# Output groups begun inside the gates' stage, and the next part's first two products begun inside each part of a feed-forward

## The chip, the cores and the metric

One core of a Trainium2 chip runs the whole program. The metric is device microseconds (us) of one execution, the median over several; the profile is of one execution more. TensorE is PE in the rows, VectorE DVE, ScalarE ACT, GpSimd POOL, SyncE SP.

## What is computed

Two transformer blocks follow each other on 1,024 tokens of width 1,024. The first has two layers. Each layer projects its input, runs four kinds of attention side by side, multiplies their joined output by a gate, projects it and normalises:

```python
for l in range(DEPTH):                      # DEPTH = 2
    proj = jnp.einsum('bsd,dc->bsc', h_res, w_in[l])
    ...
    mixed = jnp.concatenate([_merge(out_fox), _merge(out_sb), _merge(out_mla), _merge(out_mem)], axis=-1)
    y = jnp.einsum('bsc,cd->bsd', mixed * jax.nn.silu(gate), w_out[l])
    h_res = _layer_norm(DEEPNORM_ALPHA * h_res + y, ln_g[l], ln_b[l])
```

The second block has one layer, with window attention, a recurrent mixer and at the end a feed-forward of inner width 4,096:

```python
h = rms_norm(x, norm_ffn_pre[l]) * (1.0 + sc2) + sh2
f = jnp.square(jax.nn.relu(h @ w_ff1[l])) @ w_ff2[l]
x = (x + gt2 * rms_norm(f, norm_ffn_post[l])).astype(x.dtype)
```

## The kernel before

Every large product is made of three: both factors are split into a rounded high part and a low part (value minus high), and `split_gemm` (L202 to L210) adds high by high, high by low and low by high into one PSUM bank. A sum over the eight channel tiles of 128 is thus 24 matmuls. Weights come from HBM in chunks of 1 MB, by SP's queue; POOL splits each (a CAST at L193 and a TENSOR_TENSOR at L195 for the first block, L3959 and L3961 for the feed-forward).

The program is a row of stages, each an `nc.Block()`: every engine has its own instruction list for the stage, and the stage ends with a barrier at which all five engines meet. No engine starts on the next stage's list before all have come to the end of this one. SP's list opens with the clearing of the previous stage's semaphores, then issues the stage's first loads. Inside a stage the order is written out by hand, and semaphores that count finished groups tie the engines together.

**The gates' stage** (`gate_stage`, L2031, once per layer). TensorE makes 16 groups g of 24 matmuls with 512 columns: chunk c = g // 4 has four groups, tile g // 2 % 2 by half g % 2 (a half is 512 tokens), into bank g % 4. ACT takes the sigmoid of the bank (L2079), DVE multiplies it by the bank (L2094, `gated`), then into `mixed` (L2096), ACT rounds the product to `mixed_high` (L2075), and DVE makes `mixed_low` (L2088), two groups behind. SP loads the chunks C_GATE + 2, C_GATE + 3, C_OUT and C_OUT + 1 after 4, 8, 12 and 16 groups; POOL splits all but the last, which is left to the next stage.

**The edge** (`boundary`, L1178, after each layer). Out groups g = 0 to 31 (`do_out`, L1351) are 24 matmuls of 256 columns each: column chunk c = g // 4 % 4, token tile t = 4 * (g // 16) + g % 4, into bank g % 4. DVE adds each to the residual x (`add`, L1457). Here x was put away in HBM during the layer, since its place in SBUF was used for other things, and its two halves of 2 MB are the first loads of the stage (L1284). What gates group 4 is this:

```python
def room(g):
    if g >= 4:
        pe.wait_ge(*evacuated(g - 4))      # DVE's add(g - 4), which waits for x
...
if g < 16 and g % 4 == 0 and c == 1:
    pe.wait_ge(w_split, 1)                 # POOL's split of C_OUT + 1, in this stage
```

Later in the stage come statistics, normalisation (L1481, L1482) and the turn to channel-major, paced by those adds.

**The feed-forward** (`feed_forward`, L4121) runs in four parts of 1,024 inner channels, a stage each (`ffn_part`). Upward: 16 groups of 24 matmuls with 512 columns into banks g % 4, four groups to a weight chunk; groups 4 and on wait for `moved`, ACT's relu of the group four before (L4279), and each fourth for `wsplit`, POOL's split of its chunk. DVE squares (L4223) and splits. Downward: 32 groups of 12 matmuls in banks 0 to 7; DVE adds them into x_residual_two (L4235 in the first part, L4237 later; `added`). At the end of a part SP loads chunks 0 and 1 of the next (chunk 1 only when all downward groups are done), and POOL splits chunk 0, but not chunk 1. The stage before the feed-forward, `mix_out`, ends with `ffn.begin_up(0)` and `ffn.begin_up(1)`: seven of the eight channel tiles of upward groups 0 and 1, 21 matmuls each. Only the first part uses that (`begun = KT - 1 if first and g < 2`); its groups 0 and 1 are the last 3 matmuls each.

Of the kernel before, what the change touches and what calls it, by code (L numbers as in the profile page):

```python
# [31 lines left out]
P = 128  # L32
# [1145 lines left out]
def boundary(k, a, last, b):  # L1178
# [99 lines left out]
    with nc.Block() as block:  # L1278
# [63 lines left out]
        @block.tensor  # L1342
        def _(pe):
            if mem:
                pe.wait_ge(const_here, 16)

            def room(g):
                if g >= 4:
                    pe.wait_ge(*evacuated(g - 4))

            def do_out(g):  # L1351
                c, t = out_group(g)
                if g < 16 and g % 4 == 0 and c == 1:
                    pe.wait_ge(w_split, 1)
                room(g)
                gemm(nc, bank(g, 256), over_columns(last, C_OUT + c, t, 0, 256, last.mixed_high, last.mixed_low)).then_inc(products, 1)

            def do_turn(half, c):
                n = 8 * half + c
                pe.wait_ge(normed, 4 * half + 4)  # L1360
                if n >= 4:
                    pe.wait_ge(split, n - 3)
                for i in range(4):
                    mm = nc.tensor.transpose(k.psum[:, 4 + n % 4, i * P:(i + 1) * P], x[:, 4 * half + i, c * P:(c + 1) * P], k.ident)
                mm.then_inc(turned, 1)

            def do_fox(n):
                kind = fox[n][0]
                room(n_out + n)
                if kind == "logit":  # L1370
                    c, to, pairs = C_FL, bank(n_out + n)[0:FORGET_COLS, :], over_tokens(b, C_FL, 0, FORGET_COLS, fox[n][1])
                elif kind == "value":
                    c, to, pairs = C_FV, bank(n_out + n, 256), over_columns(b, C_FV, fox[n][1], 0, 256)
                else:
                    c, to = C_FQ if kind == "query" else C_FK, bank(n_out + n)
                    pairs = over_tokens(b, c, fox[n][1] * P, P, fox[n][2])
                if n < 9:
                    pe.wait_ge(w_split, (1 if last else 0) + (C_FL, C_FQ, C_FK, C_FV).index(c) + 1)
                pe.wait_ge(split, 8 if n < 9 else 16)
                gemm(nc, to, pairs).then_inc(products, 1)  # L1380

            def do_mem():
                for c in range(KT):
                    pe.wait_ge(mem_ready, 2)
                    if c >= 4:
                        pe.wait_ge(mem_moved, c - 3)
                    for t in range(2):
                        mm = nc.tensor.transpose(k.psum[:, 4 + c % 4, t * P:(t + 1) * P], mem_x[:, t, c * P:(c + 1) * P], k.ident)
                    mm.then_inc(mem_turned, 1)

            def turn_vectors():
                pe.wait_ge(rows_here, 16 * (len(vector_rows(a, vec_rows)) + 1))
                nc.tensor.transpose(k.psum[:, 4, 0:98], vec_rows, k.ident[0:98, 0:98]).then_inc(vec_turned, 1)
                nc.tensor.transpose(k.psum[:, 5, 0:32], mod_rows, k.ident[0:32, 0:32]).then_inc(vec_turned, 1)

            def turn_mix(n):
                (t0, t1), c = mix_units[n]
                pe.wait_ge(diagonal_ready, t1)
                if n >= 2:
                    pe.wait_ge(*mix_moved(n - 2))  # L1400
                for i, t in enumerate(range(t0, t1)):
                    mm = nc.tensor.matmul(k.psum[:, 6 + n % 2, i * P:(i + 1) * P], x[:, t, c * P:(c + 1) * P], diagonals[:, t, :],
                                          start=True, stop=True)
                mm.then_inc(mix_turned, 1)

            for g in range(n_out):
                if b and 22 <= g < 30:
                    do_turn(0, g - 22)
                if not b and g == 8:
                    turn_vectors()  # L1410
                if not b and 23 <= g < 31:
                    turn_mix(g - 23)
                do_out(g)
            if not b:
                for n in range(8, len(mix_units)):
                    turn_mix(n)
            if b:
                if not last:
                    for c in range(KT):
                        do_turn(0, c)  # L1420
                for n in range(9):
                    if n >= 4:
                        do_turn(1, n - 4)
                    do_fox(n)
                for c in range(5, KT):
                    do_turn(1, c)
                for n in range(9, len(fox)):
                    if mem and n == 12:
                        do_mem()
                    do_fox(n)  # L1430
# [600 lines left out]
def gate_stage(k, b, tag):  # L2031
    nc, W = k.nc, b.W
    mixed = b.mixed
    st = Stage(k, "gate" + tag)
    names = ("products_done", "sigmoid_ready", "gated", "dve_step", "weights_rounded", "weights_split", "mixed_rounded")
    products, sigmoid, gated, step, rounded, split, mixed_rounded = (st.sem(n) for n in names)
    n_groups = 2 * NT
    with nc.Block() as block:  # L2038
        @block.sync
        def _(sp):  # L2040
            st.clear_previous(sp)
            W.load(sp, C_OUT + 2)
            W.load(sp, C_OUT + 3)
            for n in range(4):

                sp.wait_ge(products, 4 * (n + 1))
                W.load(sp, C_GATE + 2 + n)

        @block.tensor
        def _(pe):  # L2050
            for g in range(n_groups):
                c = g // 4
                if g % 4 == 0 and c >= 2:

                    pe.wait_ge(split, c + 1)
                if g >= 4:

                    pe.wait_ge(gated, g - 3)
                gemm(nc, k.bank(g % 4), over_tokens(b, C_GATE + c, g // 2 % 2 * P, P, g % 2)).then_inc(products, 1)

        @block.gpsimd
        def _(pool):
            def used(c):
                if c < C_OUT + 2:
                    pool.wait_ge(products, 4 * (c - 2 - C_GATE + 1))
            W.split(pool, (C_OUT + 2, C_OUT + 3, C_GATE + 2, C_GATE + 3, C_OUT), rounded, split, used)

        def part_of(x, g):
            return x[:, g // 2, g % 2 * HALF:(g % 2 + 1) * HALF]

        @block.scalar
        def _(act):
            def round_high(g):
                act.wait_ge(step, g + 1)
                nc.scalar.copy(part_of(b.mixed_high, g), part_of(mixed, g)).then_inc(mixed_rounded, 1)  # L2075

            for g in range(n_groups):
                act.wait_ge(products, g + 1)
                nc.scalar.activation(part_of(b.gate_sigmoids, g), k.bank(g % 4), ACT.Sigmoid).then_inc(sigmoid, 1)  # L2079
                if g:  # L2080
                    round_high(g - 1)
            round_high(n_groups - 1)

        @block.vector
        def _(dve):
            def subtract(g):
                dve.wait_ge(mixed_rounded, g + 1)
                nc.vector.tensor_tensor(part_of(b.mixed_low, g), part_of(mixed, g), part_of(b.mixed_high, g), ALU.subtract)  # L2088

            for g in range(n_groups):  # L2090
                s = part_of(b.gate_sigmoids, g)
                part = part_of(mixed, g)
                dve.wait_ge(sigmoid, g + 1)
                nc.vector.tensor_tensor(s, s, k.bank(g % 4), ALU.mult).then_inc(gated, 1)  # L2094
                dve.wait_ge(gated, g + 1)
                nc.vector.tensor_tensor(part, part, s, ALU.mult).then_inc(step, 1)  # L2096
                if g >= 2:
                    subtract(g - 2)
            subtract(n_groups - 2)
            subtract(n_groups - 1)  # L2100
# [2020 lines left out]
def feed_forward(k, ffn, post, out):  # L4121
# [8 lines left out]
    def ffn_part(part, which):  # L4130
# [22 lines left out]
        with nc.Block() as block:  # L4153
# [33 lines left out]
            def _(pe):  # L4187

                for g in range(2 * KT):
                    if g % 4 == 0 and g:  # L4190
                        pe.wait_ge(wsplit, g // 4)
                    if g >= 4:

                        pe.wait_ge(moved, g - 3)
                    begun = KT - 1 if first and g < 2 else 0
                    split_gemm(nc, k.bank(g % 4), [ffn.up_product(g, i) for i in range(begun, KT)], first=not begun).then_inc(up_done, 1)

                for n in range(2):
                    for r in range(2):
# [4 lines left out]
                        for t in (4, 5, 6, 7, 0, 1, 2, 3) if not n and not r else range(NT):  # L4204
                            if not n and not r and t == 0:
                                pe.wait_ge(moved, 16)
                            if n and not r:
# [2 lines left out]
                            split_gemm(nc, k.bank(t), [((hid_high[:, 4 * r + i, tok], hid_low[:, 4 * r + i, tok]),  # L4210
                                                        weights(c, i, 0, HALF)) for i in range(4)],
                                       first=(r == 0), last=(r == 1)).then_inc(down_done, 1)

            @block.vector
            def _(dve):
# [119 lines left out]
```

## Time and profile before

| what | value |
|---|---|
| median of 3 runs | 3958.15 us (3957.75 to 3960.38) |
| the profiled execution's own time | 3959.55 us |
| its span, first to last instruction | 3957.7 us |
| granted TensorE clock, mean | 0.971 of full |
| TensorE busy | 93 % |
| VectorE busy | 44 % |
| ScalarE busy | 29 % |
| GpSimd busy | 18 % |
| data moved | 225.78 MB, 57 GB/s mean |

Shares are of the span. The 1.85 us between span and time lie around the recorded instructions. A matmul's busy time is longer than the distance to the next one's start, since matmuls are pipelined; what a group takes is its count by the distance of starts. A wait "<-PEq L2038" is idle time of TensorE that ended with its own sequencer's instruction on that line, here the barrier at a stage's end.

### The profile page before, as it was taken

What the parts mean: (1) busy time and instruction counts of PE and PEld (TensorE: products, weight loads), DVE (VectorE), ACT (ScalarE), POOL (GpSimd) and SP (SyncE); (2) the same over time, 40 slices, a digit from 0 to 9 for tenths busy, and PEclk for the clock granted to TensorE, in tenths of its full rate; (3) what the DMA queues carried; (4) which work ended last, traced back from release to release, by engine and by line L of the source; (5) the groups of instructions that cost most, each with busy time, mean ns of one, the idle gap of its engine ahead of it and who ended that gap; (6) DMA issues with size and microseconds to landing.
All of it is one profiled execution on the core that took longest, in us unless ns stands there. A gap on an engine that the chain in (4) does not pass through costs nothing. (4 is left out here: it accounts for less than half of the span.)

```text
span 3957.7 us, 67331 instructions
## 1 busy us (share of the span) xinstructions
PE 3693.3 (93%) x29462; PEld 2793.7 (71%) x29462; DVE 1733.6 (44%) x3002; ACT 1154.9 (29%) x2208; POOL 710.9 (18%) x248
## 2 busy tenths in 40 slices
PE   6899998998999989899889999998999999999998
PEld 5664667886646678778667777776687568887876
DVE  6645546456445364531774555454003253223143
ACT  2436333114363331201644444443110121001011
POOL 2110003121100041122011111110221012322321
PEclk9999899999998999999999999999899999999999
DMA  4131201221212012312110010000213211111112
GB/s 154 46 94 40 64 14 62 76 75 51 89 40 65 16 60 76 129 43 73 51 37 19 25 30 25 25 30 18 80 56 93 86 43 43 54 43 54 43 59 101
DMA packets 190189, 225.78 MB, mean 57 GB/s; under 512 B 20990, under 2 KB 168000, under 8 KB 187080
## 3 DMA queue, kind: packets, MB, share of 16 engines
q1 hardware_dynamic: 189896, 221.47, 16.9%
q8 instruction: 233, 3.82, 0.4%
q14 instruction: 60, 0.49, 0.0%
HBM read 188.89 MB, written 32.56 MB: 56 GB/s over the span
## 5 line engine op out<-in xcount | busy, mean ns | idle before, releaser
L193 POOL CAST weights_high<-weights_value 128x2048 fp32r<-128x2048 f32 x34 | 66.3, 1949 | 1260.9 <-DMA weights_value<-in_w_in_dram 1017.3
L208 PE MATMUL banks<-h_high,weights_high 128*128 128x512 f32 x608 | 242.5, 399 | 8.1 <-PEq L830 5.1
L208 PE MATMUL banks<-h_high,weights_low 128*128 128x512 f32 x608 | 239.3, 394 | 0.0
L208 PE MATMUL banks<-ffn_in_high,ffn_weights_high 128*128 128x512 f32 x512 | 202.7, 396 | 3.4 <-PEq L4153 3.1
L208 PE MATMUL banks<-ffn_in_low,ffn_weights_high 128*128 128x512 f32 x512 | 202.3, 395 | 0.0
L208 PE MATMUL banks<-ffn_in_high,ffn_weights_low 128*128 128x512 f32 x512 | 202.2, 395 | 0.0
L208 PE MATMUL banks<-ffn_weights_high,hidden_high 128*128 128x512 f32 x512 | 199.2, 389 | 0.0
L208 PE MATMUL banks<-ffn_weights_low,hidden_high 128*128 128x512 f32 x512 | 199.2, 389 | 0.0
L208 PE MATMUL banks<-ffn_weights_high,hidden_low 128*128 128x512 f32 x512 | 199.2, 389 | 0.0
L4279 ACT ACTIVATE hidden_value<-banks 128x512 f32<-128x512 f32 x64 | 38.3, 599 | 547.7 <-PE banks L208 547.6
L208 PE MATMUL banks<-h_high_again,pair_weights_high 128*128 128x512 f32 x384 | 179.5, 467 | 7.1 <-PEq L2318 7.1
L3959 POOL CAST ffn_weights_high<-ffn_weights_value 128x2048 fp32r<-128x2048 f32 x32 | 60.7, 1897 | 622.9 <-DMA ffn_weights_value<-in_w_ff_dram 445.0
L195 POOL TENSOR_TENSOR weights_low<-weights_value,weights_high 128x2048 fp32r<-128x2048 f32 x34 | 161.6, 4752 | 2.7
L4223 DVE TENSOR_TENSOR hidden_value<-hidden_value 128x512 f32<-128x512 f32 x64 | 71.2, 1114 | 200.1 <-ACT hidden_value L4279 200.1
L208 PE MATMUL banks<-weights_high,mixed_high 128*128 128x256 f32 x512 | 148.3, 290 | 8.4 <-PEq L2038 8.4
L850 PE MATMUL banks<-keys,queries 64*128 64x512 f32 (+3 forms) x512 | 110.8, 550 | 47.2 <-ACT attention_scratch L968 41.8
L208 PE MATMUL banks<-h_split_low,pair_weights_high 128*128 128x512 f32 x384 | 152.6, 397 | 0.0
L3961 POOL TENSOR_TENSOR ffn_weights_low<-ffn_weights_value,ffn_weights_high 128x2048 fp32r<-128x2048 f32 x32 | 151.7, 4739 | 2.6
L208 PE MATMUL banks<-h_high_again,pair_weights_low 128*128 128x512 f32 x384 | 150.4, 392 | 0.0
L208 PE MATMUL banks<-weights_high,h_high 128*128 128x256 f32 (+1 forms) x512 | 145.3, 284 | 1.9 <-PEq L625 1.9
L208 PE MATMUL banks<-weights_low,mixed_high 128*128 128x256 f32 x512 | 146.6, 286 | 0.0
L208 PE MATMUL banks<-weights_high,second_low 128*128 128x256 f32 (+1 forms) x512 | 145.0, 283 | 0.0
(481 smaller groups left out, 9148.1 us busy)
## 6 DMA issues: line engine op xcount, KB each, us to landing
ffn_weights_value<-in_w_ff_dram SPq DMA_DIRECT2D x32, 1024.0 KB, 5.2
weights_value<-in_w_in_dram SPq DMA_DIRECT2D x24, 1024.0 KB, 5.2
attention_scratch<-in_ada_w_dram SPq DMA_DIRECT2D x12, 1024.0 KB, 5.2
pair_weights_value<-in_w_in_dram SPq DMA_DIRECT2D x24, 512.0 KB, 4.0
ndow_weights_value<-in_w_in_dram SPq DMA_DIRECT2D x10, 1024.0 KB, 5.2
weights_value<-in_w_out_dram SPq DMA_DIRECT2D x8, 1024.0 KB, 5.0
gates_value<-in_w_in_dram SPq DMA_DIRECT2D x16, 512.0 KB, 4.6
first_mixed<-in_ada_w_dram SPq DMA_DIRECT2D x6, 1024.0 KB, 5.3
```

Of the source, the lines that this page charges most:

```text
L193: nc.gpsimd.tensor_copy(high, value).then_inc(rounded, 1)
L195: nc.gpsimd.tensor_tensor(low, value, high, ALU.subtract).then_inc(done, 1)
L208: mm = nc.tensor.matmul(out, x, y, start=(first and i == 0 and j == 0), stop=(last and i == n - 1 and j == 2))
L850: mm = nc.tensor.matmul(slot(e, at + done, size), q(p, e, t), key(p, e, done * P, (done + size) * P), start=True, stop=turned_part is None)
L3959: nc.gpsimd.tensor_copy(high[:], value[:]).then_inc(rounded, 1)
L3961: nc.gpsimd.tensor_tensor(low[:], value[:], high[:], ALU.subtract).then_inc(split, 1)
L4223: nc.vector.tensor_tensor(place(hid_value, g), place(hid_value, g), place(hid_value, g), ALU.mult).then_inc(squared, 1)
L4279: nc.scalar.activation(place(hid_value, g), k.bank(g % 4), ACT.Relu).then_inc(moved, 1)
```

## The change

In the gates' stage the groups of a chunk change places: both tiles of half 0 come first, then both of half 1, and `part_of` follows. After group 15 TensorE goes on, in the same stage, with 21 of the 24 matmuls (channel tiles 0 to 6) of out groups 0 to 3, into banks 0 to 3 with 256 columns. It waits for the split of C_OUT (`split`, 5), for `mixed_low` of group 12 (a new semaphore `mixed_split`, 13) and for each bank's gating. In the edge's stage groups 0 to 3 keep their last 3 matmuls each. In the feed-forward each part but the last ends with `begin_up` of the next part's groups 0 and 1, after waits for the split of the next chunk 0 (`wsplit`, 8) and for DVE's adds of banks 0 and 1, and all four parts start groups 0 and 1 with the last 3 matmuls. No load, no split and no other engine's work changes, except that SP clears one semaphore more per layer. The number of matmuls is the same.

```diff
--- before.py
+++ after.py
@@ -1353,7 +1353,9 @@
                 if g < 16 and g % 4 == 0 and c == 1:
                     pe.wait_ge(w_split, 1)
                 room(g)
-                gemm(nc, bank(g, 256), over_columns(last, C_OUT + c, t, 0, 256, last.mixed_high, last.mixed_low)).then_inc(products, 1)
+                begun = KT - 1 if g < 4 else 0
+                split_gemm(nc, bank(g, 256), over_columns(last, C_OUT + c, t, 0, 256, last.mixed_high, last.mixed_low)[begun:],
+                           first=not begun).then_inc(products, 1)
 
             def do_turn(half, c):
                 n = 8 * half + c
@@ -2032,8 +2034,8 @@
     nc, W = k.nc, b.W
     mixed = b.mixed
     st = Stage(k, "gate" + tag)
-    names = ("products_done", "sigmoid_ready", "gated", "dve_step", "weights_rounded", "weights_split", "mixed_rounded")
-    products, sigmoid, gated, step, rounded, split, mixed_rounded = (st.sem(n) for n in names)
+    names = ("products_done", "sigmoid_ready", "gated", "dve_step", "weights_rounded", "weights_split", "mixed_rounded", "mixed_split")
+    products, sigmoid, gated, step, rounded, split, mixed_rounded, mixed_split = (st.sem(n) for n in names)
     n_groups = 2 * NT
     with nc.Block() as block:
         @block.sync
@@ -2056,7 +2058,12 @@
                 if g >= 4:
 
                     pe.wait_ge(gated, g - 3)
-                gemm(nc, k.bank(g % 4), over_tokens(b, C_GATE + c, g // 2 % 2 * P, P, g % 2)).then_inc(products, 1)
+                gemm(nc, k.bank(g % 4), over_tokens(b, C_GATE + c, g % 2 * P, P, g // 2 % 2)).then_inc(products, 1)
+            pe.wait_ge(split, 5)
+            pe.wait_ge(mixed_split, n_groups - 3)
+            for t in range(4):
+                pe.wait_ge(gated, n_groups - 3 + t)
+                split_gemm(nc, k.bank(t, 256), over_columns(b, C_OUT, t, 0, 256, b.mixed_high, b.mixed_low)[:KT - 1], last=False)
 
         @block.gpsimd
         def _(pool):
@@ -2066,7 +2073,8 @@
             W.split(pool, (C_OUT + 2, C_OUT + 3, C_GATE + 2, C_GATE + 3, C_OUT), rounded, split, used)
 
         def part_of(x, g):
-            return x[:, g // 2, g % 2 * HALF:(g % 2 + 1) * HALF]
+            tile, half = g // 4 * 2 + g % 2, g // 2 % 2
+            return x[:, tile, half * HALF:(half + 1) * HALF]
 
         @block.scalar
         def _(act):
@@ -2085,7 +2093,8 @@
         def _(dve):
             def subtract(g):
                 dve.wait_ge(mixed_rounded, g + 1)
-                nc.vector.tensor_tensor(part_of(b.mixed_low, g), part_of(mixed, g), part_of(b.mixed_high, g), ALU.subtract)
+                nc.vector.tensor_tensor(part_of(b.mixed_low, g), part_of(mixed, g), part_of(b.mixed_high, g),
+                                        ALU.subtract).then_inc(mixed_split, 1)
 
             for g in range(n_groups):
                 s = part_of(b.gate_sigmoids, g)
@@ -4192,7 +4201,7 @@
                     if g >= 4:
 
                         pe.wait_ge(moved, g - 3)
-                    begun = KT - 1 if first and g < 2 else 0
+                    begun = KT - 1 if g < 2 else 0
                     split_gemm(nc, k.bank(g % 4), [ffn.up_product(g, i) for i in range(begun, KT)], first=not begun).then_inc(up_done, 1)
 
                 for n in range(2):
@@ -4210,6 +4219,11 @@
                             split_gemm(nc, k.bank(t), [((hid_high[:, 4 * r + i, tok], hid_low[:, 4 * r + i, tok]),
                                                         weights(c, i, 0, HALF)) for i in range(4)],
                                        first=(r == 0), last=(r == 1)).then_inc(down_done, 1)
+                if not last:
+                    pe.wait_ge(wsplit, 8)
+                    for g in range(2):
+                        pe.wait_ge(added, NT + g + 1)
+                        ffn.begin_up(g)
 
             @block.vector
             def _(dve):
```

TensorE's list at the end of the first gates' stage, before; the branch is the end of the stage's list, and the next one waits for the barrier:

```order
L208 MATMUL banks<-second_low,weights_high 128x512
L208 MATMUL banks<-h_high,weights_low 128x512
L2038 UNCONDITIONAL_BRANCH
L1342 UNCONDITIONAL_BRANCH [waits barrier_Pool_Activation_PE_DVE_SP_release]
L208 MATMUL banks<-weights_high,mixed_high 128x256
```

and with the change. The names of semaphores that the listing prints are those of the first stage that had the same numbers; the waits here are for `split`, `mixed_split` and `gated`:

```order
L208 MATMUL banks<-second_low,weights_high 128x512
L208 MATMUL banks<-h_high,weights_low 128x512
L208 MATMUL banks<-weights_high,mixed_high 128x256 [waits fox_0_late_values_done,fox_0_scaled,fox_0_act_moved]
L208 MATMUL banks<-weights_low,mixed_high 128x256
L208 MATMUL banks<-weights_high,first_low 128x256
```

Out group 0 has moved ahead of the barrier. Its and its three followers' 84 matmuls end here, at what is left of group 0 behind the barrier:

```order
L208 MATMUL banks<-weights_low,mixed_high 128x256
L208 MATMUL banks<-weights_high,first_low 128x256
L2040 UNCONDITIONAL_BRANCH
L1342 UNCONDITIONAL_BRANCH [waits barrier_Pool_Activation_PE_DVE_SP_release]
L208 MATMUL banks<-weights_high,mixed_high 128x256
L208 MATMUL banks<-weights_low,mixed_high 128x256
L208 MATMUL banks<-weights_high,first_low 128x256
```

Twelve matmuls stand behind the barrier where 96 stood, and then group 4 with its two waits, for DVE's add of group 0 and for POOL's split of C_OUT + 1:

```order
L208 MATMUL banks<-weights_low,mixed_high 128x256
L208 MATMUL banks<-weights_high,first_low 128x256
L208 MATMUL banks<-weights_high,mixed_high 128x256 [waits fox_0_max_ready,sb_project_0_condition_biased]
L208 MATMUL banks<-weights_low,mixed_high 128x256
L208 MATMUL banks<-weights_high,first_low 128x256
```

Only the distance from the barrier to this row is changed; the row stood, with both waits, 96 matmuls behind the barrier.

TensorE's list between the first two parts of the feed-forward, before:

```order
L208 MATMUL banks<-ffn_weights_low_30586,hidden_high 128x512
L208 MATMUL banks<-ffn_weights_high_30582,hidden_low 128x512
L4153 UNCONDITIONAL_BRANCH
L4186 UNCONDITIONAL_BRANCH [waits barrier_Pool_Activation_PE_DVE_SP_release]
L208 MATMUL banks<-ffn_in_high,ffn_weights_high_30581 128x512
```

and with the change (the two waits are `wsplit` and `added`):

```order
L208 MATMUL banks<-ffn_weights_low_30600,hidden_high 128x512
L208 MATMUL banks<-ffn_weights_high_30596,hidden_low 128x512
L208 MATMUL banks<-ffn_in_high,ffn_weights_high_30595 128x512 [waits latent_heads_0_values_done,latent_heads_0_latents_turned]
L208 MATMUL banks<-ffn_in_low,ffn_weights_high_30595 128x512
L208 MATMUL banks<-ffn_in_high,ffn_weights_low_30599 128x512
L208 MATMUL banks<-ffn_in_high,ffn_weights_high_30595 128x512
```

The upward products of the next part have moved ahead of the barrier, 42 matmuls; three each of groups 0 and 1 stay behind it.

## Rows read from the trace of the kernel before

**Rows 1.** Part 1 of the page: busy us (share of the span) and instructions of TensorE.

```profile
PE 3693.3 (93%) x29462; PEld 2793.7 (71%) x29462; DVE 1733.6 (44%) x3002; ACT 1154.9 (29%) x2208; POOL 710.9 (18%) x248
```

**Rows 2.** What TensorE waited for, whole span: line, releaser, us in total, times, longest.

```profile
PE banks L208 <- PEq L2038: 8.4, 2, 4.2
...
PE banks L208 <- PEq L4153: 3.1, 3, 1.1
...
PE banks L208 <- PEq L3992: 0.3, 1, 0.3
```

**Rows 3.** Timeline, first edge (gates to output): start us, us, engine, line, [idle before <-releaser].

```profile
723.50 0.69 DVE L2088 TENSOR_TENSOR first_low<-first_mixed,mixed_high 128x512 fp32r<-128x512 f32 x1
...
726.71 0.39 PE L208 MATMUL banks<-h_high,weights_low 128*128 128x512 f32 x1
...
729.10 1.89 DVE L2088 TENSOR_TENSOR first_low<-first_mixed,mixed_high 128x512 fp32r<-128x512 f32 x3
...
731.65 0.82 SPq L1284 DMA_DIRECT2D second_value<-x_waiting  x2
...
732.08 1.89 POOL L193 CAST weights_high<-weights_value 128x2048 fp32r<-128x2048 f32 x1 [15.82 <-DMA weights_value<-in_w_out_dram]
...
734.05 4.57 POOL L195 TENSOR_TENSOR weights_low<-weights_value,weights_high 128x2048 fp32r<-128x2048 f32 x1
```

**Rows 4.** Timeline of DVE, first output groups after that edge.

```profile
739.02 0.99 DVE L1457 SCALAR_TENSOR_TENSOR second_value<-second_value,banks 128x256 f32<-128x256 f32 x2 [8.03 <-DMA second_value<-x_waiting]
...
748.07 0.42 DVE L1457 SCALAR_TENSOR_TENSOR second_value<-second_value,banks 128x256 f32<-128x256 f32 x1 [2.41 <-PE banks L208]
```

**Rows 5.** Stretches after a wait: window us, busy us (xcount) by engine, PEclk, DMA share, GB/s.

```profile
731.30:737.30 6.00, 6.00 (x31) 6.00 (x32) 0.00 (x0) 1.24 (x1) 5.14 (x2) 0.56 0.82 300
...
1519.40:1525.40 6.00, 6.00 (x30) 6.00 (x31) 0.00 (x0) 1.21 (x1) 5.12 (x2) 0.53 0.82 303
```

**Rows 6.** Timeline, second edge.

```profile
1514.79 0.39 PE L208 MATMUL banks<-h_high,weights_low 128*128 128x512 f32 x1
...
1519.72 0.34 SPq L1284 DMA_DIRECT2D x_residual<-x_waiting  x1
...
1527.05 0.42 DVE L1457 SCALAR_TENSOR_TENSOR x_residual<-x_residual,banks 128x256 f32<-128x256 f32 x1 [7.99 <-DMA x_residual<-x_waiting]
...
1536.51 0.42 DVE L1457 SCALAR_TENSOR_TENSOR x_residual<-x_residual,banks 128x256 f32<-128x256 f32 x1 [2.46 <-PE banks L208]
```

**Rows 7.** Stretches of TensorE's clock after longer waits, columns as in rows 5.

```profile
2020.20:2026.20 6.00, 5.99 (x20) 4.83 (x21) 1.79 (x6) 2.55 (x3) 0.00 (x0) 0.74 0.43 129
...
3220.90:3226.90 6.00, 6.00 (x35) 5.92 (x35) 3.02 (x4) 2.60 (x4) 4.39 (x1) 0.67 0.98 335
...
469.00:494.00 25.00, 23.48 (x90) 12.52 (x92) 13.77 (x28) 7.30 (x19) 3.88 (x1) 0.50 0.00 1
```

**Rows 8.** Timeline of TensorE where those longer waits end.

```profile
2020.21 0.77 PE L208 MATMUL banks<-h_high_again,pair_weights_high 128*128 128x512 f32 x1 [7.14 <-PEq L2318]
...
3220.89 1.43 PE L4023 MATMUL banks<-hidden_value,x_residual_two 128*128 128x128 f32 x5 [6.59 <-DVE hidden_value L4099]
```

**Rows 9.** Timeline, edge between the first two parts of the feed-forward.

```profile
3407.42 0.69 DVE L4235 COPY x_residual_two<-banks 128x512 f32<-128x512 f32 x1 [2.03 <-PE banks L208]
...
3408.43 0.47 PE L208 MATMUL banks<-ffn_in_high,ffn_weights_high 128*128 128x512 f32 x1 [1.05 <-PEq L4153]
...
3392.99 4.60 POOL L3961 TENSOR_TENSOR ffn_weights_low<-ffn_weights_value,ffn_weights_high 128x2048 fp32r<-128x2048 f32 x1
...
3412.70 1.90 POOL L3959 CAST ffn_weights_high<-ffn_weights_value 128x2048 fp32r<-128x2048 f32 x1 [15.11 <-DMA ffn_weights_value<-in_w_ff_dram]
...
3419.91 0.60 ACT L4279 ACTIVATE hidden_value<-banks 128x512 f32<-128x512 f32 x1 [5.00 <-PE banks L208]
...
3425.51 0.60 ACT L4279 ACTIVATE hidden_value<-banks 128x512 f32<-128x512 f32 x1 [4.49 <-PE banks L208]
```

**Rows 10.** Timeline, mix_out to the first part: TensorE arrives last at that edge.

```profile
3240.27 0.47 PE L208 MATMUL banks<-ffn_in_high,ffn_weights_high 128*128 128x512 f32 x1 [0.30 <-PEq L3992]
```

## The prediction

> **What bounds the kernel now.** I read the page first, then TensorE's waits, the timeline at each edge that the change touches, and the granted clock behind it. TensorE is busy 93 % of the span [rows 1], so what counts is where it idles and how fast it is clocked. Among its waits three are the change's: 8.4 us in two, 4.2 each, at the barrier behind the gates' stage, and 3.1 us in three, some 1.05 each, at the barriers between parts of the feed-forward [rows 2]. The fourth barrier there, behind mix_out, costs 0.3 us; there TensorE itself comes last, with products begun for the next stage, which is the state that the change makes everywhere.
>
> At the first gates' edge TensorE's last matmul ends at 727.10 and DVE's last subtraction at 730.99; TensorE starts again at 731.3, SP issues the load of x at 731.65, POOL starts splitting C_OUT + 1 at 732.08 [rows 3]. DVE's first add starts at 739.02, released by x [rows 4]. TensorE doesn't feel that: it has 96 matmuls of groups 0 to 3 to do, some 14 us. It does pay for the pause in clock: over the 6 us from 731.3 the mean clock is 0.56, over the 6 from 1519.4 it is 0.53 [rows 5]. With levels 0.5 and 1 (1.2 and 2.4 GHz) that is 2 x 6 x (1 - 0.56) = 5.28 us low at the first edge and 5.64 at the second.
>
> Distances of starts: a group of 24 matmuls with 256 columns takes 2.41 + 0.42 = 2.83 us, 0.118 each [rows 4], at the second edge 2.88, 0.120 each [rows 6]. Low, it is some 25 matmuls in 5.28 us, 0.211 each: the first window of rows 5 has 31, of which 0.72 us at 0.118 make 6. A microsecond low thus loses 1 - 0.118 / 0.211 = 0.44. With 512 columns a group takes 5.60 us, 0.233 each [rows 9].
>
> **The gates' edge.** Nothing is removed from any list but the order; the sum of matmuls is the same. *Begun groups:* 84 matmuls now follow the last gate group at once. None of their waits bites: C_OUT was split 15.82 us before 732.08 [rows 3], the low part of group 12 is ready at 723.50 + 0.69, and the fourth bank, gated before 729.10, is wanted only after 63 matmuls. They start at 726.71 + 0.23 = 726.94, take 84 x 0.118 = 9.91, and the last ends 0.16 later (0.39 less 0.23) at 737.01. All engines but TensorE have then been done for 6 us, so TensorE opens the barrier. *The load of x:* it stands behind the barrier. SP issued it 0.66 after the last arrival (731.65 - 730.99); with one semaphore more to clear I take 0.71, so 737.72. DVE could add 739.02 - 731.65 = 7.37 us behind the issue, so now 745.09. *TensorE* meanwhile has 12 matmuls, 1.4 us, and then stands at group 4, whose bank needs DVE's add of group 0: 745.09 + 0.42 + 0.05 = 745.56. What is queued behind that wait is the whole rest of the stage, and DVE's adds, the statistics and the normalisation with it. POOL's split, which also starts at the barrier, takes 734.05 + 4.57 - 732.08 = 6.54 and is done by 737.01 + 0.3 + 6.54 = 743.85: it waits too, but not last. *Against before:* DVE's add of group 4 began at 748.07. Now 745.56 + 2.83 + 0.20 (0.16 as above and 0.04 from TensorE's end to DVE's start, 3407.42 against 3408.43 - 1.05 [rows 9]) = 748.59, **0.52 later** at full clock. The second edge likewise [rows 6]: 1514.79 + 0.23 + 84 x 0.120 + 0.16 + 0.71 = 1525.97, plus 1527.05 - 1519.72 = 7.33 gives 1533.30, plus 0.42 + 0.05 + 2.88 + 0.20 = 1536.85 against 1536.51, **0.34 later**. So the old wait of 4.2 us goes, and a wait of 745.56 - 738.7 = 6.9 us behind the barrier comes in its place.
>
> *Clock:* the pause is no shorter, so the clock should fall again. The nearest rows are waits of 7.14 us and 6.59 us [rows 8], behind which the mean over 6 us is 0.74 and 0.67, 3.12 and 3.96 us low [rows 7]; at 0.44 that loses 1.37 and 1.74, mean 1.56. The old loss is in the old times already. Bounds: nothing, if the clock stays, and 5.64 x 0.44 = 2.5, as long as behind the old pause. I take 1.56 at each edge, as those waits are nearest in length.
>
> Both edges: 0.52 + 0.34 + 2 x 1.56 = **4.0 us lost**. Could x come earlier? Before, it shared the queue with the end of the load of C_OUT + 1, which landed 0.43 after x was issued; at most that much is gained, and with no clock loss the edge costs nothing: 0 to 3.0 each. The new order inside the gates' stage I cost at nothing: TensorE waits for nobody in that stage but through `gated`, with the same lag of four groups.
>
> The Trainium skill has a rule that speaks against this change, DMA: Bandwidth & Descriptors, section "Rules for kernel authors": issue a DMA early, do compute, and wait late. The change takes 84 matmuls of compute from between issue and wait. [...]
>
> **The feed-forward.** At the first edge TensorE's last matmul ends at 3407.38, DVE adds for 0.69, TensorE goes on at 3408.43 [rows 9]. Now 42 matmuls, 9.8 us, follow at once. Chunk 0 of the next part is split by 3392.99 + 4.60 = 3397.59, and banks 0 and 1 were added seven groups ago. TensorE then opens the barrier and pays what it pays behind mix_out, 0.30 [rows 10]. Gain 1.05 - 0.30 = 0.75, three times: **2.25 us won**; bounds 3 x 1.05 = 3.15 and nothing. The next wait to be late would be POOL's split of chunk 1, which starts behind the barrier: 3417.3 + 6.5 = 3423.8, wanted by group 4 after 6 matmuls and two groups, at 3417.3 + 1.4 + 11.2 = 3429.9, so 6 us to spare. Before, it started at 3412.70, when its load had landed. The clock doesn't fall at these edges (1.05 us), so nothing is won on it.
>
> **Sum.** 4.0 - 2.25 = +1.75. The profiled execution took 3959.55 us (span 3957.7), so 3961.3 by it; the median is 1.4 lower, so **3959.9 us**.
>
> **The rivals.** *Edges filled:* TensorE finds x in time. Then both pauses of 4.2 go down to 0.3 and the clock losses of 5.28 and 5.64 us at 0.44 (4.8) with them: 7.8 + 4.8 + 2.25 = 14.9 us won, 3943.3. For it: that's how the feed-forward's edges go. Against: x is issued behind the barrier and takes 7.3 us against 1.4 us of work. It would take a landing under 2 us. Chance 0.05.
>
> *The clock stays down:* behind a wait of under 5 us the clock was low for at least 25 us on end, 469 to 494 [rows 7]. If that happens behind one new wait of 6.9 us, it costs 25 x 0.44 = 11.0 in place of 1.56: 3969.3, slower. It decides from about 17 us on: (3966.1 - 3959.9 + 1.56) / 0.44. Against: in those 25 us TensorE issued only 90 matmuls, here it issues one each 0.211 us, and four restarts like that were low for 3.1 to 5.6 us. Chance 0.06.
>
> *No gain in the feed-forward:* the barrier costs 1.05 with TensorE last too. Then 3962.2, no change. Chance 0.06. That begun groups wait in the gates' stage and so do nothing is excluded by the margins above.
>
> **How the numbers follow.** The forecast has 0.83. Its own range: edges 0 to 6.0, feed-forward -3.15 to 0, so 3955.0 to 3964.2, and the three runs lay 0.4 under and 2.2 over their median: 3954.5 to 3965.5. 0.2 % of this kernel, 7.9 us, is what a measurement can tell from no change: 3950.2 to 3966.1 is "same". Faster is the first rival, slower the second, with a hundredth more for what I have not seen.
>
> **What would show it.** Right: DVE's first add of each edge is still released by x, some 8.1 us behind TensorE's last matmul before the barrier; TensorE has a wait of 6 to 7 us in the edge's stage, ended by DVE's add (or, by 1.7 us, by POOL's split), and none of 4.2 at the barrier; the clock is low behind it for 3 to 6 us; DVE's add of group 4 comes 1 to 3 us later behind the last gate matmul than before; waits between parts are 0.3. Wrong: group 4 starting within 3 us of the barrier, or a clock that doesn't fall, or a new wait in the feed-forward at group 4.

## The result

Over 16 executions of each kernel the change took 3968.68 us (3959.45 to 3970.69) against 3962.05 (3957.75 to 3965.1); the ratio is 1.0013, 95 % interval 1.0007 to 1.0019. By the ratio that is 5.2 us slower (2.8 to 7.5); the two medians differ by 6.6 us, and 1.75 us were forecast. The measured time lies outside the range given, 3954.5 to 3965.5. It is 8.8 us over the forecast of 3959.9. Of these, 3.9 are the level: the three runs shown of before had a median of 3958.15, and that of the sixteen is 3962.05. The rest, 4.9 us by the medians and 3.4 by the ratio, is the change's own, and the sections below are about it.

The profiled execution of the change took 3961.18 us, span 3959.4. The page's busy times and the waits of TensorE over the whole span, against [rows 1, 2]:

```profile
PE 3689.9 (93%) x29462; PEld 2793.1 (71%) x29462; DVE 1733.7 (44%) x3002; ACT 1155.2 (29%) x2208; POOL 712.3 (18%) x248
```

```profile
PE banks L208 <- DVE x_residual L1459: 6.7, 1, 6.7
...
PE banks L208 <- DVE second_value L1459: 6.7, 1, 6.7
...
PE banks L208 <- PEq L4162: 0.9, 3, 0.3
...
PE banks L208 <- PEq L2040: 0.6, 2, 0.3
```

The 8.4 us at the barrier behind the gates are 0.6 now, and the 3.1 us between the parts of the feed-forward are 0.9. In their place stand two waits of 6.7 us for DVE's add (L1459 here is L1457 of before). The first edge in order of time, against [rows 3, 4]; ACT's row is the last gate sigmoid, which starts as TensorE's last gate matmul ends, and serves as the zero of time at each edge:

```profile
725.44 0.60 ACT L2087 ACTIVATE gate_sigmoids<-banks 128x512 f32<-128x512 f32 x1 [4.50 <-PE banks L208]
```

```profile
735.59 1.89 POOL L193 CAST weights_high<-weights_value 128x2048 fp32r<-128x2048 f32 x1 [20.42 <-POOLq L2040]
...
737.56 4.49 POOL L195 TENSOR_TENSOR weights_low<-weights_value,weights_high 128x2048 fp32r<-128x2048 f32 x1
```

```profile
736.03 0.81 SPq L1284 DMA_DIRECT2D second_value<-x_waiting  x2
```

```profile
743.41 1.42 DVE L1459 SCALAR_TENSOR_TENSOR second_value<-second_value,banks 128x256 f32<-128x256 f32 x4 [14.11 <-DMA second_value<-x_waiting]
...
748.53 0.42 DVE L1459 SCALAR_TENSOR_TENSOR second_value<-second_value,banks 128x256 f32<-128x256 f32 x1 [3.71 <-PE banks L208]
```

SP issues x 10.6 us behind the last gate group, POOL's split ends at 742.05, x releases DVE at 743.41, and the four adds that had piled up run in one go. DVE's add of group 4 comes 748.53 - 725.44 = 23.1 us behind the sigmoid; before it was 748.07 - 727.13 = 20.9. The clock behind the two waits, with columns as in [rows 5]:

```profile
744.00:750.00 6.00, 6.00 (x39) 6.00 (x40) 1.94 (x5) 0.00 (x0) 0.00 (x0) 0.73 0.97 398
...
1530.60:1536.60 6.00, 5.99 (x31) 6.00 (x32) 1.44 (x5) 0.00 (x0) 0.00 (x0) 0.58 0.96 394
```

By the two levels of the prediction, half and full, it is low for 12 x (1 - 0.73) = 3.2 us at the first edge and for 5.0 at the second.

This one profile agrees with the forecast to 0.1 us: 3961.18 - 3959.55 = 1.63. The sixteen executions don't; the profiled one is the second shortest of them. So the question of the experiments was what the profile of one execution didn't show.

### The profile page after: what moved, and what is told of

Same layout as the page of the kernel before. It is cut to its first block and busy times, and to the rows that moved or that the text cites. A ratio compares the mean times of both kernels' runs of the same rounds, so it can differ in the third digit from the quotient of the medians.

```text
span 3959.4 us, 67338 instructions
## 1 busy us (share of the span) xinstructions
PE 3689.9 (93%) x29462; PEld 2793.1 (71%) x29462; DVE 1733.7 (44%) x3002; ACT 1155.2 (29%) x2208; POOL 712.3 (18%) x248
```

## The experiments

All ratios are to the kernel before, run beside it on the same chip, with 95 % intervals; e1 to e4, e5 to e8 and e9 to e12 ran on one chip each. For the edges one figure is compared: from the start of the last gate sigmoid (ACT) to the start of DVE's add of group 4, at the first and the second edge, read from each profile as above.

| kernel | ratio | interval | first edge, us | second edge, us |
|---|---|---|---|---|
| before, first profile | 1 | | 20.9 | 21.3 |
| e5 before again | 0.9997 | 0.9988 to 1.0006 | 21.3 | 21.5 |
| e3 feed-forward only | 0.9996 | 0.9987 to 1.0005 | 20.1 | 21.4 |
| e9 no group begun | 0.9997 | 0.9988 to 1.0006 | 20.1 | 21.3 |
| the change | 1.0013 | 1.0007 to 1.0019 | 23.1 | 24.1 |
| e1 the change again | 1.0014 | 1.0006 to 1.0023 | 24.0 | 24.1 |
| e2 gates only | 1.0022 | 1.0013 to 1.0030 | 23.7 | 23.9 |
| e6 new wait filled | 1.0000 | 0.9992 to 1.0009 | 21.4 | 21.7 |
| e8 old pause filled | 0.9988 | 0.9979 to 0.9997 | 18.6 | 18.8 |
| e4 x early | 0.9997 | 0.9988 to 1.0006 | 21.2 | 21.5 |
| e7 x and split early | 0.9971 | 0.9961 to 0.9980 | 17.8 | 16.4 |
| e12 three begun | 1.0001 | 0.9992 to 1.0010 | 21.8 | 22.0 |
| e11 two begun | 0.9992 | 0.9981 to 1.0002 | 20.6 | 19.5 |
| e10 one begun | 0.9979 | 0.9970 to 0.9988 | 17.1 | 17.2 |

### The change again, and its two parts

The change as it is:

> The change as it is, timed anew and profiled anew. Its first profile has the forecast edges (a wait of 6.7 us before group 4 at each) and 0.3 us between the parts of the feed-forward, and its profiled execution took 1.63 us more than the one of before (3961.18 against 3959.55); but over 16 executions each the ratio is 1.0013, some 5.2 us. Theory A, the clock behind the new wait is luckier in that profile than in most executions: a second profile has the same waits and a longer low clock at one of the edges or elsewhere, ratio again 1.0010 to 1.0017. Theory B, the first profile is typical and the 16 executions were spread over unequal conditions: ratio 1.0003 to 1.0006.

Only the gates' part, that is the change without

```diff
-                    begun = KT - 1 if g < 2 else 0
+                    begun = KT - 1 if first and g < 2 else 0
...
-                if not last:
-                    pe.wait_ge(wsplit, 8)
-                    for g in range(2):
-                        pe.wait_ge(added, NT + g + 1)
-                        ffn.begin_up(g)
```

> Only the gates' part of the change; the feed-forward is as before. If the parts add up and the feed-forward wins 2.25 us, this is 2.25 us slower than the whole change: ratio to before 1.0010 by the first profile, some 1.0018 by the timed ratio. If the feed-forward's part is what costs the unexplained 3.5 us (theory C), this is faster than the whole change: ratio 1.0005 or less.

Only the feed-forward's part (the same lines added to the kernel before):

> Only the feed-forward's part; the gates' stage and the edge are as before. By the profile of the change: three waits of 1.05 us become 0.3, so 2.25 us faster, ratio 0.9994. Theory C (it costs): 1.0004 or more.

The change again: 3966.88 us against 3960.96, ratio 1.0014. Gates only: 1.0022. Feed-forward only: 0.9996, with an interval that takes in both no change and twice the forecast. The two parts multiply to 1.0018, inside the interval of the whole. Theory C falls: the feed-forward's part doesn't cost. The three waits of the barriers between its parts, in the profile of e3:

```profile
PE banks L208 <- PEq L4153: 0.9, 3, 0.3
```

3.1 - 0.9 = 2.2 us, as forecast to 0.1. In the profile of e2 they are still there, 3.1 us. So all of the loss is in the gates' part, and it is some 2.2 + 5.2 = 7 to 9 us (1.0022 is 8.7) where 4.0 were forecast.

The second profile of the change (span 3966.2) has the same two waits, 6.74 and 6.66 us, and this clock behind them:

```profile
745.40:751.40 6.00, 6.00 (x31) 6.00 (x32) 1.34 (x5) 0.00 (x0) 0.00 (x0) 0.56 0.96 395
...
1537.30:1543.30 6.00, 5.96 (x31) 5.99 (x32) 1.37 (x5) 0.00 (x0) 0.00 (x0) 0.56 0.99 407
```

5.3 us low at each. Theory A stands, and mostly by its "or elsewhere". The clock at the first edge makes 24.0 - 23.1 = 0.9 of the 6.8 us between the two spans (3966.2 - 3959.4). Most of them lie where the change touches nothing: from DVE's add of group 4 at the first edge to the last gate sigmoid of the second layer the first profile took 763.3 us and the second 767.9; the first profile of before took 767.1. So it was luck that the first profile met the forecast to 0.1 us. In the profile of e2 the clock is low for 4.7 and 4.9 us. The mean of these six is 4.7 us, not the 3.5 of the two waits from which I took the price.

### The kernel before, again

> The kernel before, profiled again. It tells how much of a difference between two profiles is the profiles' own. In the four profiles of the changed edges each edge costs 2.2 to 3.1 us against the one profile of before, and the stretches behind the edges, which the change doesn't touch, gain or lose up to 5 us, wherever a pause of 2.6 to 2.9 us is or isn't met by a fall of the clock. If that is chance, this profile differs from the first of before by some us outside the edges, and its edges cost the same as in the first, 20.9 to 21.4 us from ACT's last gate sigmoid to DVE's add of group 4. If it is brought on by the change, this profile equals the first within 1 us everywhere.

Its edges are 21.3 and 21.5, close to the first profile; the span is 3960.1 against 3957.7, so profiles of one kernel do differ by some us. The first edge is 20.1 in e3 and e9, with the same pause of 4.2 us: the mean clock of the 6 us behind it is 0.72 in both, 0.56 in the first profile of before and 0.50 in e5. Much of what differs between profiles is thus chance, but not all of it falls evenly. Behind the second edge, from DVE's add of group 16 to that of group 31, five profiles (before, e5, e3, e9, e4) take 53.0 us, and the three of the change and of e2 take 54.4, 54.4 and 55.8. What differs is one pause that the change doesn't touch. Here are TensorE's wait and the 6 us behind it in the first profile of before:

```profile
1591.36 0.82 PE L1402 MATMUL banks<-mem_channel_major,x_residual 128*128 128x128 f32 x5 [2.60 <-DVE mem_channel_major L1556]
```

```profile
1591.40:1597.40 6.00, 6.00 (x51) 6.00 (x52) 1.90 (x3) 0.78 (x1) 0.00 (x0) 1.00 0.01 3
```

and in that of the second profile of the change:

```profile
1597.61 0.80 PE L1404 MATMUL banks<-mem_channel_major,x_residual 128*128 128x128 f32 x2 [2.60 <-DVE mem_channel_major L1558]
```

```profile
1597.40:1603.40 6.00, 5.79 (x38) 5.80 (x39) 0.53 (x2) 0.78 (x2) 0.00 (x0) 0.74 0.01 3
```

The same pause of 2.60 us, once without and once with a fall of the clock (12 x 0.26 = 3.1 us low), worth 1.3 us of the distance above; in e2, with the mean clock at 0.50, it was worth 2.8. The clock fell there in the first profile of the change too, and in those of e7, e8, e10 and e12, and not in e6 and e11: in seven of fourteen profiles. e8 has the gates and the groups of before, e4 and e6 those of the change, so the fall isn't bound to the change's edge. Whether the change makes it more likely, a few profiles can't say.

### Filling the new wait, and filling the old pause

The whole change, with 56 extra matmuls behind the rest of group 3. Their product isn't used:

```diff
                 do_out(g)
+                if g == 3:
+                    for i in range(56):
+                        nc.tensor.matmul(k.bank(7, 256), last.h_high[:, i % 8, 0:P], last.h_high[:, i % 8, 0:256], start=True, stop=True)
```

> The whole change, with 56 extra matmuls of 256 columns (6.6 us at full clock) behind what is left of groups 0 to 3, into a bank that is free there. They compute nothing that is used, and end just before the wait of 6.7 us would; so the wait stays but the clock's fall is taken away. Theory (the new wait costs its clock loss too): faster than the whole change by 2.3 us at each edge, 4 to 5 us, ratio to before 1.0002. Rival (the clock loss is small or the extra matmuls delay group 4): no faster than the whole change, 1.0013 or more.

The kernel before, with 32 extra matmuls behind the last gate group:

```diff
                 gemm(nc, k.bank(g % 4), over_tokens(b, C_GATE + c, g // 2 % 2 * P, P, g % 2)).then_inc(products, 1)
+            for i in range(32):
+                nc.tensor.matmul(k.bank(7, 256), b.h_high[:, i % 8, 0:P], b.h_high[:, i % 8, 0:256], start=True, stop=True)
```

> The kernel before, with 32 extra matmuls of 256 columns (3.8 us at full clock) behind the last gate group, ahead of the barrier, into a free bank. They compute nothing that is used and end when DVE's last subtraction does; the pause of 4.2 us becomes one of 0.3. It prices the clock loss of the old pause by itself: 0.44 x 5.3 and 0.44 x 5.6, so 4.8 us faster, ratio 0.9988. If the clock's fall is of no account, 1.0000.

Both came out as the theory has it. With useless work in the wait of 6.7 us the clock doesn't fall, in these 9 us nor in the 10 behind them:

```profile
736.00:745.00 9.00, 8.96 (x75) 8.99 (x76) 1.41 (x4) 1.28 (x1) 6.50 (x2) 1.00 0.88 346
```

The second edge has 1.00 as well, and DVE's add of group 4 comes at 21.4 and 21.7 us instead of a mean of 23.6 and 24.0: 2.2 and 2.4 us of clock loss at each edge. Against before, 20.6 and 21.4 on the mean of the four profiles with its edges (before, e5, e3, e9), 0.8 and 0.3 us are left, near the 0.52 and 0.34 of the forecast. The ratio goes from 1.0014 to 1.0000, some 5 us; the two intervals overlap a little (1.0006 to 1.0023 and 0.9992 to 1.0009), so it is the edges that show the step. In the kernel before the same trick is worth 20.6 - 18.6 = 2.0 and 21.4 - 18.8 = 2.6 us, ratio 0.9988 (0.9979 to 0.9997), the 4.8 us that were expected. So the old pause of 4.2 us and the new one of 6.7 lose about the same in clock.

### x early, and x and the split early

The whole change, with SP's loads of x moved to the end of the gates' stage, and their wait in the edge's stage on the new semaphores:

```diff
                 sp.wait_ge(products, 4 * (n + 1))
                 W.load(sp, C_GATE + 2 + n)
+                if n == 3:
+                    for half in range(2):
+                        sp.dma_start(b.after[:, 4 * half:4 * half + 4, :], k.x_home[:, 4 * half:4 * half + 4, :]).then_inc(b.x_early[half], 16)
```

> The whole change, with the two loads of x moved from behind the barrier to the end of the gates' stage, behind the load of C_OUT + 1 (their place is free once the 16 gate groups are done). POOL's split of C_OUT + 1 stays behind the barrier. x then lands about when the barrier opens, and group 4 waits for POOL's split, which ended 6.5 us behind the barrier: its wait becomes some 5.0 us in place of 6.7, so 1.5 us won at each edge, 3 us in all, ratio to before 1.0005 if the whole change has 1.0013. If it is x alone that holds group 4 and the split doesn't matter, the wait goes away altogether, and with it two clock losses: ratio under 0.9970.

TensorE at the first edge:

```profile
PE banks L208 <- POOL weights_low L195: 4.8, 1, 4.8
```

x is there, and the next in line holds group 4, POOL's split, for 4.8 us (5.0 expected). The ratio is 0.9997, where 1.0005 was expected; the interval takes in both. The edges came 2.4 and 2.5 us earlier than the mean of the change's, and not 1.5: besides the wait, which is 1.9 us shorter, the clock is low for 12 x (1 - 0.74) = 3.1 and 12 x (1 - 0.72) = 3.4 us, at the short end of what stands behind the change's own waits (3.2 to 5.3). That a shorter wait does this isn't shown by two stretches. The first of them:

```profile
744.00:750.00 6.00, 5.95 (x38) 5.95 (x39) 1.11 (x2) 0.00 (x0) 1.14 (x3) 0.74 0.19 38
```

With the split moved as well:

```diff
-            W.split(pool, (C_OUT + 2, C_OUT + 3, C_GATE + 2, C_GATE + 3, C_OUT), rounded, split, used)
+            W.split(pool, (C_OUT + 2, C_OUT + 3, C_GATE + 2, C_GATE + 3, C_OUT, C_OUT + 1), rounded, split, used)
...
-                last.W.split(pool, (C_OUT + 1,), w_rounded, w_split)
```

> The whole change, with the loads of x and POOL's split of C_OUT + 1 moved into the gates' stage. TensorE ends its begun groups 10.1 us behind the last gate group; POOL's split ends at about 5.2 + 6.5 = 11.7 and opens the barrier, x has landed at about 12.5. So TensorE pauses some 2 us at the barrier and 1 us at group 4, in place of 0.3 and 6.7, and the clock mostly stays. Against the whole change 4 us less waiting and 2.3 us less clock loss at each edge: 12 us, ratio to before 0.9985. If something else stands ready to hold group 4 (the adds, the room in the banks), the gain is that of the x load alone, 0.9997 as timed in the run with x early.

```profile
PE banks L208 <- PEq L2035: 1.9, 1, 1.9
```

One pause of 1.9 us is left at the first edge, 1.7 at the second, at the barrier that POOL now opens, and none at group 4. Ratio 0.9971 (0.9961 to 0.9980), 3950.41 us against 3962.11: the fastest kernel of the study, 11.7 us under before by the medians. That is more than the 0.9985 expected: 3 us of waiting were expected to be left at each edge, and there were 1.9 and 1.7. The clock fell behind the first pause (0.72 over 6 us) and not behind the second, which is why the edges are 17.8 and 16.4.

### How many groups to begin

The change with `range(4)` and `g < 4` at none, 1, 2 and 3, here for one:

```diff
-                begun = KT - 1 if g < 4 else 0
+                begun = KT - 1 if g < 1 else 0
...
-            for t in range(4):
+            for t in range(1):
```

> The change with no output group begun in the gates' stage: the new order of the gates and the feed-forward's part stay. If the order of the gates costs nothing, the edges are as before (20.8 and 21.4 us from the last gate sigmoid to DVE's add of group 4) and the ratio is that of the feed-forward's part alone, 0.9996. If the order has a part in the loss: 1.0000 or more.

> One output group begun in place of four. TensorE ends it 2.5 us behind the last gate group, before DVE's last subtraction, which still opens the barrier 4.2 us behind; the pause is 1.7 us and the clock should stay. Behind the barrier there are 75 matmuls, 8.9 us, more than x takes (7.7 us from the barrier), so no wait at group 4. By the times of the first profile of before DVE's add of group 4 comes at 731.3 + 99 x 0.118 + 0.2 = 743.2 against 748.07, 4.9 us earlier, 5.0 at the second edge; with the feed-forward 12 us, ratio 0.9969. Rival (the pause, not the load of x, is what the begun groups fill, so fewer win less than four): above 1.0000.

> Two output groups begun. TensorE opens the barrier 5.0 us behind the last gate group, and has 54 matmuls, 6.4 us, behind it against 8.6 us until DVE has added group 0: a wait of some 2 us at group 4, too short for the clock to fall. DVE's add of group 4 at 740.6 + 3.0 = 743.6 against 748.07, 4.4 us earlier, 4.7 at the second edge; with the feed-forward 11 us, ratio 0.9971.

> Three output groups begun. The barrier opens 7.5 us behind the last gate group, 33 matmuls, 3.9 us, stand behind it, and the wait at group 4 is 4.5 us, long enough for the clock to fall (the old pause of 4.2 was). DVE's add of group 4 at 743.1 + 3.0 + 2.2 of clock loss = 748.3, as before; with the feed-forward 2 us won: ratio 0.9995. If the clock stays in spite of 4.5 us: 0.9984.

None begun: 0.9997, as with the feed-forward's part alone (0.9996), and the edges of before, so the new order of the gates costs nothing that these runs can see. Then 0.9979, 0.9992, 1.0001 and, with four, 1.0014. The intervals of neighbours overlap, but the edges go the same way, 17.1, 20.6, 21.8 and, on the mean of three, 23.6 us at the first: each group more than the first makes it slower. With one begun, DVE still opens the barrier, and TensorE has two short waits at the first edge, with the clock at 1.00 through the 10 us behind the barrier:

```profile
PE banks L208 <- PEq L2040: 1.7, 1, 1.7
...
PE banks L208 <- DVE second_value L1459: 0.8, 1, 0.8
```

```profile
731.60:741.60 10.00, 9.20 (x76) 9.06 (x77) 0.69 (x3) 1.28 (x1) 6.51 (x2) 1.00 0.88 346
```

One and two fell short of what was expected of them (0.9969 and 0.9971), for the load of x took longer than in the profiles before:

```profile
732.06 0.81 SPq L1284 DMA_DIRECT2D second_value<-x_waiting  x2
```

```profile
740.91 1.41 DVE L1459 SCALAR_TENSOR_TENSOR second_value<-second_value,banks 128x256 f32<-128x256 f32 x4 [9.60 <-DMA second_value<-x_waiting]
```

From issue to DVE's first add 8.85 us, not 7.37. With two begun it was 8.86 and 8.74, so the wait at group 4 was 3.2 and 3.0 us and not 2, and the clock fell behind it (0.51 and 0.75 over 6 us). With three, 8.05 and 7.88; waits 4.9 and 4.7, and a ratio of 1.0001, whose interval (0.9992 to 1.0010) holds the 0.9995 expected. Why the load took longer wasn't tried.

## Why the prediction was wrong

**Right.** The mechanism at the edges: that the begun groups run without a wait, that TensorE then opens the barrier, that x stands behind it and takes as long as before, that group 4 waits 6 to 7 us (6.7) for DVE's add, and POOL's split is done before it (742.05; x releases the adds at 743.41). The lateness without the clock, 0.52 and 0.34: e6 has 0.8 and 0.3. The feed-forward: 2.25 forecast, 2.2 in the waits of e3, with nothing late behind it. The order of the gates at nothing (e9). None of the three rivals came. That the first profile's total met the sum was luck, as said under e1.

**Wrong: the term for the clock.** The step that failed is the price of the clock's fall behind the new wait: "I take 1.56 at each edge, as those waits are nearest in length." e6 against the change gives 2.2 and 2.4. The two waits of [rows 8] are near in length, but the stretch that runs low depends on more than the length of the wait: behind those two it was 3.1 and 4.0 us, behind the six new ones 3.2 to 5.3, mean 4.7. And one reading of a wait is no price. Behind the very same wait of 7.1 us (L2318 of before), with the same matmuls behind it, the clock is low for 2.8 to 6.0 of the next 6 us in the fourteen profiles, mean 3.6; behind the wait of 6.6 us it is 3.8 to 5.3, mean 4.5. The profile of before had 3.1 and 4.0, both under the mean. At its longest, in e2 behind 7.07 us, with columns as in [rows 7]:

```profile
2027.80:2033.80 6.00, 6.00 (x14) 4.73 (x15) 1.77 (x6) 2.55 (x3) 0.00 (x0) 0.50 0.43 128
```

At the prediction's 0.44 the mean of 4.7 us costs 2.1, near what e6 gives, so what was mis-sized is the low time and not its price. The upper bound that I gave, 2.5 as behind the old pause, was nearly the value; it was the row with the same matmuls at the same place. The edges thus cost, on the mean of three profiles of the change's edges (its two and e2's) and four of before's, 23.6 - 20.6 = 3.0 and 24.0 - 21.4 = 2.6, 5.6 us, and not 4.0.

**Missing: what lies behind.** 5.6 - 2.2 = 3.4 us, against 5.2 timed (2.8 to 7.5). The interval allows 3.4 alone. The profiles show one more cost, the fall of the clock at the pause of 2.60 us behind the second edge, in all three profiles with the change's edges and in none of the four with those of before: 1.3, 1.3 and 2.8 us, mean 1.8. With it the account is 5.2. I had a term for no stage that the change doesn't touch. Whether this fall is bound to the displacement or three coin tosses isn't settled, and with other stretches that vary by several us from profile to profile (the one between the edges takes 763.3 to 769.5 us in the fourteen) it is partly luck that the account closes.

**The range** held the sum's bounds (at most +6.0, and the measured +5.2 is under it), but stood on three runs of before, whose median was 3.9 us lower than that of the sixteen. The spread of three runs was taken for the spread of all. The range was also added up wrong at its upper end: 3964.2 + 2.2 is 3966.4, not 3965.5. The measured time lies outside either.

## What to carry to other kernels

Work moved ahead of a barrier moves the barrier too, once its engine is the last to arrive, and with it every load and every split that stands behind it. Count the work that is left between the barrier and the first wait on such a load: here the load needs 8 us and four begun groups left 1.4 us of work, one begun group left 8.9. Begin as much as fills the pause and no more, or issue the load ahead of the barrier, together with whatever is next in line: with x alone moved, POOL's split still held TensorE for 4.8 us. A pause of this length (4.2 us before, 6.7 after) cost its clock loss again where it was moved to. Price that with the row that has the same instructions behind it, and from more than one profile: the same wait differed by 3 us of low clock between profiles.

## What the runs showed of the hardware

The clock's fall behind a pause can be bought off with matmuls that compute nothing, 2.0 to 2.6 us for each pause of 4.2 to 6.7 us (e6, e8). Behind one wait of 7.1 us, the same in fourteen profiles, the clock was low for 2.8 to 6.0 us. A pause of 2.60 us was met by a fall in seven profiles and not in the other seven, with the same instructions around it; pauses of 1.7 us were not (e10, both edges, and e7's second), and one of 1.9 us was (e7's first).

The same load of 2 MB, issued first in its stage, released DVE 7.1 to 7.4 us after its issue in most profiles, after 8.7 to 8.9 with one or two groups begun (both edges of both), after 8.1 and 7.9 with three, and after 8.5 at one edge of e8 and 7.4 at the other. In the slow ones of e8 and e10 TensorE worked at full clock while the load ran, but so it did at the other edge of e8 and in e6, where the load took 7.1 and 7.2. The cause wasn't tried.
